# Mixture-of-experts layer on Trainium2: one wide expert and two small ones interleaved by weight halves

## The reference

```python
logits = t @ w_router + b_router
top_vals, top_idx = lax.top_k(logits, 2)
gates = sum(one_hot(top_idx, 8) * softmax(top_vals)[..., None], axis=1)
for e in range(8):
    out += gates[:, e:e+1] * ((silu(t @ w_gate[e]) * (t @ w_up[e])) @ w_down[e])
```

## Time and profile before

| | |
|---|---|
| runs | 1678.63, 1679.26, 1683.75 us (median 1679.26) |
| profiled execution | 1676.72 us, span 1675.0 us |
| TensorE | 1592.3 us busy, mean granted clock 0.973 |
| VectorE, ScalarE | 1271.2 us, 1008.1 us |
| read from HBM | 461.15 MB, 276 GB/s over the span |
| narrow items | 7, from 559.6 us on |
| wide item | matmuls from 1439.6 to 1653.7 us |

### The profile page before, as it was taken

The page is one execution under the profiler, slowest core; times in us unless marked ns, Lnnn a source line. Parts: engine busy times, 40 slices in busy tenths (PEclk is TensorE's granted clock), DMA queues, the critical chain, the costliest instruction groups (busy, mean ns, idle before and its releaser), DMA issues.

```text
span 1675.0 us, 24350 instructions
## 1 busy us (share of the span) xinstructions
PE 1592.3 (95%) x9043; PEld 1346.6 (80%) x9043; DVE 1271.2 (76%) x1389; ACT 1008.1 (60%) x1010; POOL 217.0 (13%) x251
## 2 busy tenths in 40 slices
PE   6988999997989799999999999999999999899996
PEld 4766899997678688888888888888888888788785
DVE  4895476656864898898898898888988988555454
ACT  4555555453134677777777877777776876444442
POOL 0770155531930000000000000000000000000000
PEclk9998999998999899999999999999999999999998
DMA  9954386664666699999999999999999996466531
GB/s 300 339 202 141 124 283 215 214 215 161 241 212 224 249 356 372 341 365 368 339 364 371 349 344 380 341 355 378 337 361 369 338 366 223 142 210 203 199 126 38
DMA packets 231196, 463.16 MB, mean 277 GB/s; under 512 B 18255, under 2 KB 57687, under 8 KB 231127
## 3 DMA queue, kind: packets, MB, share of 16 engines
q1 hardware_dynamic: 229591, 461.55, 77.9%
q10 hardware_dynamic: 1536, 0.68, 0.2%
HBM read 461.15 MB, written 1.05 MB: 276 GB/s over the span
## 4 chain that ended last, share of the span: by engine, by line
PE 85%; DVE 5%; POOL 4%; ACT 3%; DMA 1%; issue 1%; SPq 1%; ACTq 0%; DVEq 0%; POOLq 0%
PE bank L1984 16%; PE bank L1981 16%; PE bank L1987 16%; PE bank L1641 11%; PE bank L1796 3%; PE bank L2061 2%; PE bank L2062 2%; PE bank L2069 2%; PE bank L2074 2%; PE bank L2073 2%; DVE bank L1221 2%; PE bank L1725 1%; PE bank L1947 1%; PE bank L1629 1%; PE bank L2027 1%; DMA ring<-in_mod_w_dram 1%
## 5 line engine op out<-in xcount | busy, mean ns | idle before, releaser
L1492 DVE TENSOR_TENSOR wlo<-ring,whi 128x2048 fp32r<-128x2048 f32 x294 | 667.7, 2289 | 95.1 <-PE bank L1987 76.8
L981 ACT ACTIVATE whi<-ring 128x2048 fp32r<-128x2048 f32 x294 | 561.2, 1918 | 163.7 <-PE bank L1984 163.6
L1981 PE MATMUL bank<-whi,xe_hi 128*128 128x512 f32 x784 | 307.3, 392 | 5.4 <-ACT whi L981 5.4
L1984 PE MATMUL bank<-whi,xe_lo 128*128 128x512 f32 x784 | 306.7, 391 | 0.0
L1987 PE MATMUL bank<-wlo,xe_hi 128*128 128x512 f32 x784 | 209.8, 390 | 0.0
L1981 PEld LDWEIGHTS bank<-whi,xe_hi 128*128 128x128 f32 x784 | 147.8, 189 | 36.2 <-issue 5.6
L1984 PEld LDWEIGHTS bank<-whi,xe_lo 128*128 128x128 f32 x784 | 147.9, 189 | 30.5
L1987 PEld LDWEIGHTS bank<-wlo,xe_hi 128*128 128x128 f32 x784 | 147.6, 188 | 30.6
L1552 DVE TENSOR_TENSOR wlo<-ring,whi 128x2048 fp32r<-128x2048 f32 x42 | 96.2, 2292 | 95.1 <-PE bank L2074 94.2
L1981 PE MATMUL bank<-whi,hh 128*128 128x512 f32 x392 | 157.4, 402 | 0.0
L1984 PE MATMUL bank<-whi,hl 128*128 128x512 f32 x392 | 153.4, 391 | 0.0
(11 more groups left out here) (408 smaller groups left out, 2535.4 us busy)
## 6 DMA issues: line engine op xcount, KB each, us to landing
ring<-in_moe_w_gate_dram SPq DMA_DIRECT2D x112, 1024.0 KB, 7.2
ring<-in_moe_w_up_dram SPq DMA_DIRECT2D x112, 1024.0 KB, 7.2
ring<-in_moe_w_down_dram SPq DMA_DIRECT2D x112, 1024.0 KB, 6.9
ring<-in_mod_w_dram SPq DMA_DIRECT2D x24, 2048.0 KB, 10.0
ring<-in_ffn_w_gate_dram SPq DMA_DIRECT2D x11, 1024.0 KB, 6.4
ring<-in_ffn_w_up_dram SPq DMA_DIRECT2D x11, 1024.0 KB, 8.8
ring<-in_ffn_w_down_dram SPq DMA_DIRECT2D x11, 1024.0 KB, 5.0
ring<-in_conv_w_pw_dram SPq DMA_DIRECT2D x8, 1024.0 KB, 11.8
```

Source lines behind the costliest of these rows:

```text
L981: act.activation(whi[:, n % HI_SLOTS, :], ring[:, s * HW:(s + 1) * HW], ACT.Copy).then_inc(hi_ready, 1)
L1492: v.tensor_tensor(wlo[:, n % LO_SLOTS, :], ring[:, s * HW:(s + 1) * HW], whi[:, n % HI_SLOTS, :].bitcast(F32), ALU.subtract).then_inc(lo_r ...
L1981: mm(o[:, :], xh, hi[:, w:w + 512], start=first, stop=False)
L1984: ins = mm(o[:, :], xl, hi[:, w:w + 512], start=False, stop=False)
```

## The change

The wide item becomes a trio: the wide expert and two experts of at most 64 rows, interleaved by halves.

- The order `TRIO` has 126 halves. Two halves of a small expert and one wide half alternate; at four places there are two such pairs, at four none. The small experts follow one another (expert "1", then "2"), each as U, D of the block before, G. The wide one goes U, G for all blocks, then D. The three experts share `ring` with 6 slots (`TRIO_SLOTS`), `whi` and `wlo`.
- A small expert's rows lie like the wide one's last rows: high parts in columns 0 to 63, low parts in 64 to 127 (`xs`, and `hs` for hidden values). A half has 4 steps of 2 matmuls (with `whi`, with `wlo`), 8 in all.
- The halves of a PSUM result (partitions 0 to 63 and 64 to 127) are no longer added by `fold` on TensorE: ScalarE copies the upper 64 partitions to SBUF (`uT`, `gT`, `uBt`, `gBt`), VectorE adds the lower ones (`sums`), ScalarE takes Silu in place and VectorE multiplies (`hidden_rows`); then TensorE transposes (`transposes`, two halves after the gate block's end), ScalarE makes the high part (`act_high`) and VectorE the low one (`dve_low`).
- The small experts' rows are gathered after the first wide half (`small_gather`), their selections transposed then too. The first small expert's output is scattered during the trio, the second's before the last wide half, where TensorE waits for `wide_yl`.
- The router picks the first fitting expert and the first two small ones, expert 0 excepted, and takes the trio only if all three exist; otherwise all run as narrow items. It has nine more small operations.
- At the end the order of the last output's operations changes, and an `Abs_reciprocal_sqrt` on two values is put ahead of the wait for `acc`.

```diff
-            with sp.If(wide > 0):
-                e = sp.value_load(order_i[0:1, bass.ds(narrow, 1)], min_val=0, max_val=NE - 1)
-                for n in range(NH):
-                    sp.wait_ge(lo_ready, last * NH + (NH + n + 1 - (RAW_SLOTS if n < WIDE_SLOTS else WIDE_SLOTS)))
-                    half(e, n, WIDE_HALVES, WIDE_SLOTS)
+                three = [sp.value_load(order_i[0:1, bass.ds(row + k, 1)], min_val=0, max_val=NE - 1) for k in range(3)]
+                for q, (o, kind, j, h) in enumerate(TRIO):
+                    sp.wait_ge(lo_ready, last * NH + (NH + q + 1 - (RAW_SLOTS if q < TRIO_SLOTS else TRIO_SLOTS)))
+                    half(three[o], kind, j, h, q % TRIO_SLOTS)
...
+def trio_halves():
+    wide = [(0, kind, j, h) for j in range(FT) for kind in "UG" for h in range(2)]
+    wide += [(0, "D", j, h) for j in range(FT) for h in range(2)]
+    pairs, out = small_pairs(), []
+    for n, w in enumerate(wide):
+        take = 2 if n in (14, 28, 33, 35) else 0 if n < 2 or n in (NH - 3, NH - 1) else 1
+        for _ in range(take):
+            e, kind, j = pairs.pop(0)
+            out += [(e, kind, j, 0), (e, kind, j, 1)]
+        out.append(w)
...
+            def small_product(q, i, e, kind, j, h):
+                pe.wait_ge(hi_ready, i * NH + (q + 1))
+                hi, lo = whi[:, q % HI_SLOTS, :], wlo[:, q % LO_SLOTS, :]
+                steps = small_steps(e, kind, j, h)
+                for k, (o, x, w, first, last) in enumerate(steps):
+                    if k == len(steps) - 1:
+                        pe.wait_ge(lo_ready, i * NH + (q + 1))
+                    ins = mm(o[:, :], x, hi[:, w:w + 512], start=first, stop=False)
+                ins.then_inc(hi_used, 1)
+                for o, x, w, first, last in steps:
+                    ins = mm(o[:, :], x, lo[:, w:w + 512], start=False, stop=last)
+                ins.then_inc(lo_used, 1)
...
+            def hidden_rows(q, i):
+                o, kind, j = AFTER[q]
+                if o == 0:
+                    v.wait_ge(s_ready, i * FT + (j + 1))
+                    if j:
+                        v.wait_ge(trio_t, GI[(0, j - 1)])
+                    v.tensor_tensor(hid_e[:, :], silu_g[:, :], uA[:, :], ALU.mult).then_inc(he_ready, 1)
+                sums(q, i)
...
+                v.wait_ge(sum_silu, GI[(o, j)])
+                v.tensor_tensor(a_, a_, b_, ALU.mult).then_inc(sum_hid, 1)
...
+                    if q in T_AT:
+                        transposes(T_AT[q], i)
+                    if q == SMALL_END[2] + 1:
+                        pe.wait_ge(wide_y, 4)
+                        for m in range(4):
+                            small_scatter(2, m, psum[SPARE_BANKS[m]])
...
+            act.activation(fin_scrap[:, :], ones[:, 0:2], ACT.Abs_reciprocal_sqrt)
+            act.wait_ge(acc_half, wide * 12 + NCOMB)
```

More of the change, by code:

```diff
@@ L158 @@
 GATHER_AFTER = {AT[("D", FT - 3, 1)]: 0, AT[("D", FT - 2, 1)]: 1}
-MIN_NARROW, MAX_NARROW = NE - 1, NE + 2
+MIN_NARROW, MAX_NARROW = NE - 3, NE + 3
 MAX_ROWS = NE + 4
 TAIL = 64
[L164 to L173, removed]
@@ L174, with small_pairs @@
-SPARE_BANKS = (0, 2, 6, 7)
-WIDE_EXTRA = (1, 3, 5, 4)
-WIDE_OUT = (1, 5, 3, 4)
+TRIO_SLOTS = 6
+def small_pairs():
+    first = [(1, "U", 0), (1, "G", 0)]
+    for j in range(1, FT):
+        first += [(1, "U", j), (1, "D", j - 1), (1, "G", j)]
+    second = [(2, "G", 0)]
+    for j in range(1, FT):
+        second += [(2, "U", j), (2, "D", j - 1), (2, "G", j)]
+    return first + [(2, "U", 0), (1, "D", FT - 1)] + second + [(2, "D", FT - 1)]
+def trio_halves():
[8 more added lines that the diff above has]
+        out.append(w)
+    assert not pairs
+    return out
@@ L178 @@
+T_AT = {QEND[x] + T_OFFSET[x]: x for x in G_ENDS}
+assert len(T_AT) == len(G_ENDS) and list(T_AT.values()) == G_ENDS
+UA, UB, GA, GB, SG, SU, SD = 0, 2, 6, 7, 1, 3, (5, 4)
+SPARE_BANKS = (SG, SU) + SD
+WIDE_EXTRA = SPARE_BANKS
+WIDE_OUT = (UA, UB, GA, GB)
+SMALL_END = {e: QEND[(e, "D", FT - 1)] for e in (1, 2)}
+assert SMALL_END[2] == NQ - 3
 MAGIC = 1.5 * 2.0 ** 23
@@ L516, in _, with half @@
                     sp.dma_start(early(n, 4)[:, 0:2, :], src.rearrange("(k p) n -> p k n", p=P)).then_inc(a, 16)
[L518 to L521 removed]
+            def half(e, kind, j, h, s):
                 e1 = bass.ds(e, 1)
@@ L1403, in _ @@
             link(v.tensor_scalar(r(10), r(10), -1000.0, None, ALU.add))
[L1405 to L1408, removed]
+            over, member, fits, small = rt[:, 0, 0, :], rt[:, 0, 1, :], rt[:, 1, 0, :], rt[:, 1, 1, :]
+            upto, uptosmall, first, two = rt[:, 3, 0, :], rt[:, 3, 1, :], rt[:, 4, 0, :], rt[:, 4, 1, :]
+            gone, rest, keep, uptorest = rt[:, 2, 0, :], rt[:, 2, 1, :], rt[:, 6, 0, :], rt[:, 7, 0, :]
+            tail, main, place_3 = rt[:, 7, 1, :], rt[:, 8, 0, :], rt[:, 8, 1, :]
+            any_fit, there, without, narrow = (rt[:, 5, 0, n:n + 1] for n in range(4))
             link(v.tensor_scalar(over, psum[6][:, 256:256 + NE], float(P), None, ALU.is_gt))
             link(v.tensor_scalar(fits, psum[6][:, 256:256 + NE], float(P + TAIL), None, ALU.is_le))
+            link(v.tensor_scalar(small, psum[6][:, 256:256 + NE], float(TAIL), None, ALU.is_le))
             v.wait_ge(consts, 6)
@@ L1423, in _ @@
[L1423 to L1428 removed]
+            link(v.scalar_tensor_tensor(two, uptosmall, 2.0, small, ALU.is_le, ALU.mult))
@@ new lines, in _ @@
+            link(v.tensor_scalar(without, rt[:, 2, 0, NE - 1:NE], -1.0, float(NE), ALU.mult, ALU.add))
+            link(v.tensor_tensor(narrow, without, rt[:, 7, 0, NE - 1:NE], ALU.add))
+            link(v.tensor_tensor(main, iota_e[:, :], gone, ALU.subtract))
+            link(v.tensor_tensor(place_3, two, uptosmall, ALU.mult))
+            link(v.scalar_tensor_tensor(place_3, place_3, narrow, main, ALU.add, ALU.subtract))
+            link(v.tensor_tensor(place_3, place_3, member, ALU.mult))
```

483 lines of the change are left out of this document (324 added, 159 removed).

## The result

The changed kernel takes 1614.4 us (1611.6 to 1618.5) against 1679.0 us, a ratio of 0.9615 with a 95% interval of 0.9599 to 0.9632; forecast were 1615 us and a range of 1592 to 1648. Timed again on another chip it gave 0.9612 (0.9598 to 0.9625). The profiled execution took 1611.64 us, its span is 1608.9 us.

A forecast was written before the change was run, and what follows sets the result against it. TensorE was taken to bound both stages. Trio work of 367.3 us plus 29.5 us of stalls replaces 460.8 us, gaining 64.0: 1676.7 becomes 1612.7 us profiled, with 2.5 us for the median 1615 us; range 1592 to 1648 us.

The forecast's parts named there:

- TensorE's work: In the trio: wide and small halves, transposes, gathers, scatters and a slow-clock start, 367.3 us without stalls.
- rival 4: In the trio the queue is the bound, holding 340 GB/s: about 1625 to 1640 us; chance 0.06.
- rival 2: In the trio loads average out over the buffers, stalls under 15 us: 1585 to 1600 us; chance 0.15.
- The stalls: In the trio, TensorE's holes worked out by the order of instructions: 29.5 us in all.
- Wide gates: End of a wide gate block: a 5.1 us chain against 3.6 us of TensorE work, 1.5 us late, 7 times, 10.5 us.
- small gates: End of a small gate block: sum, Silu and product outlast the gap, 0.5 us late, 14 times, 7 us.
- double pairs: Four places with four small halves in a row: VectorE 9.2 us against TensorE 7.3, 1.9 us late each, 7.5 us.
- the steady unit: Two small halves and a wide one: the second small low part, 2.29 us, fits in 2.5 us, 0.2 us to spare.
- The pause before the last wide half: Before the last wide half TensorE waits for the second small output's low parts: 2.5 us.
- rival 3: In the trio gaps pass 2.2 us and the clock falls: 27 us more, 1642 us; chance 0.18.
- The ring: Six load slots in the trio: a load has 11 us against a median 7.2 us to land, so it is covered.
- Router and end: Nine more router operations before the first high part cost 1.8 us; the reordered end saves 1.9 us; together 0.

The follow-up runs named there:

- experiment 1: Changed kernel with a third matmul in each step of a small half (12 instead of 8, no packing gain): 1662.4 us.
- 3: Changed kernel with only half the columns of each small half's low part made: 1590.0 us.
- 2: Changed kernel with only half of each small half's 1 MB loaded: 1613.0 us.
- 4: Changed kernel in a coarser order, two wide halves and then four small ones: 1628.8 us.
- early: Changed kernel with a small gate block's copy and sum made one half earlier: 1606.2 us, ratio 0.9567 to the kernel before.
- experiment 5: Changed kernel with its halves not interleaved, packing kept: 1745.9 us.
- experiment 6: Changed kernel with a ring of three slots in the trio instead of six: 1718.0 us.
- allthree: Changed kernel with wide gate row sums before hid_e, wide transposes three halves behind, small gate copy and sum one half earlier: 1605.8 us, ratio 0.9558 to the kernel before.

## Why the prediction was right

The mechanism held, and the time, 1614.4 us against 1615, is nearer than the terms deserve: several were off by 2 to 5 us, and two waits that the trace shows had no price at all. They happened to cancel.

**What bounds.** Right. TensorE's work plus holes behind VectorE: experiments 1 and 3 show the two parts, 2 rules out the queue (rival 4), 4 and 3 rule out an averaging over the buffers (rival 2).

**TensorE's work.** A small half takes 1.81 us, 1274.17 to 1275.98 in the trace, as forecast (1.82). The 64-row transposes cost 0.32 us for four instead of 0.48, so the transposes are 28 x 0.12 + 84 x 0.08 = 10.1 us instead of 13.4. The small gathers took 3.7 us; forecast were 4.0, by luck: the earlier trace rows has 16 such products in 1.98 us, not 8, and the trio makes 32 of them, not 16. Their eight transposes took 0.9 us (1.0), and the first wide halves ran at 0.72 of the clock from 1193 to 1199, 1.7 us lost as forecast. The work is thus about 364 us against 367.3.

**VectorE.** 346 us in the trio against 358 to 363. Its low parts take the 283 us of the lower forecast; the additions are 63 us where I had 75, in part because operations one behind the other start 0.61 us apart (1265.65 and 1266.26 above) and not the 0.68 us of their rows.

**The stalls.** 396.4 - 364 = 32 us against 29.5: the sum holds better than its terms.
- Wide gates: 7 waits of 1.7 us on the weight loads, 11.9 us, against 10.5. Right, and so was the chain behind it.
- Low parts: 20.9 us in 39 waits on the weight loads, against 7 us at the small gates and 7.5 at the double pairs. Behind a wait the next load comes sooner (1302.41 to 1302.52, 0.11 us instead of 0.227) and gives part of it back; so counted, the low parts delay the stream by about 15 us. The sum holds, its parts don't:
  - Twenty-two waits of 0.38 or 0.39 us, 8.4 us and about 5 us of delay, are ones in which VectorE had stood idle ahead of the low part. It waited for the end of the wide half, and no sum or split stood in its way:

```profile
1299.57 0.39 PE L2270 MATMUL bank<-wlo,xb 128*128 128x512 f32 x1
1300.07 2.29 DVE L1744 TENSOR_TENSOR wlo<-ring,whi 128x2048 fp32r<-128x2048 f32 x1 [1.73 <-PE bank L2270]
1302.41 0.19 PEld L2302 LDWEIGHTS bank<-whi,xs 128*128 128x128 f32 x1 [0.39 <-DVE wlo L1744]
```

  This is the step of the prediction that failed: the steady unit was to have 0.2 us to spare and cost nothing. I had started the low part together with the first small half. It starts 0.50 us after the wide half's last matmul and that small half's first weight load (both 1299.57), so it is made 2.79 us after them, where TensorE asks for it after 2.5 us.
  - The four double pairs: 4.8 us in eight waits against 7.5. Six waits are of 0.5 us, as the two here; at two of the places the first of them is 0.6 and 1.1 us:

```profile
1513.54 0.19 PEld L2302 LDWEIGHTS bank<-whi,xs 128*128 128x128 f32 x1 [0.51 <-DVE wlo L1744]
...
1515.74 0.19 PEld L2302 LDWEIGHTS bank<-whi,xs 128*128 128x128 f32 x1 [0.52 <-DVE wlo L1744]
```

  I had let VectorE begin the run of four with nothing made ahead (9.2 us against 7.3); the first low part is made while the wide half still runs, so that three remain, 6.9 us against the 3 x 1.82 + 0.7 = 6.2 us after which TensorE asks for the last.
  - Behind the small gate blocks: six waits of 0.6 to 1.6 us, 5.9 us, against 14 of 0.5; taking that work out of the way there (`early`) gave 5.1 us. The last three of the 39, 1.8 us, come behind sums, splits and outputs of other blocks.
- Small transposes (L2318): 5.4 us in 19 waits for which the profile names no cause, and 1.2 us in two for `gT`. The prediction has no term for them.
- The start, priced at 2 us: TensorE waited for nothing behind the first wide half and its gathers.
- The pause before the last wide half: 0.73 us against 2.5. The outputs were read out (`y_exp`, 1579.20) while the wide half before it ran; their low parts followed behind a weight's low part from 1582.60, and TensorE began at 1583.40 with the first of them.

**Clock.** No stall fell under rival 3: the longest wait of TensorE between two halves is 1.7 us, and the clock is 1.00 from 1205 to 1587. The gaps of 2.17 us and more that it fell behind in the earlier trace rows didn't come. Experiments 5 and 6, with waits of TensorE of up to 6.4 and 4.2 us, show what comes with them: mean clocks of 0.89 and 0.91. But the length of a gap isn't a sure sign, and the margin was not as clear as I had it: see the last section.

**The ring.** Six slots cover, three don't (experiment 6). Landing took a median of 6.9 to 7.2 us in the trio, as in the earlier trace rows.

**Router and end.** The router's list is right: from the table load before it to the one behind it ScalarE's rows are 13.2 us apart before (546.37 and 559.59) and 15.0 after (545.87 and 560.89), +1.8 us. The +1.3 us above has 0.5 us less from the stages ahead in it. -2.4 and -0.6 us against -1.9 for the end. The table load did move: ScalarE does it at 1594.53 while TensorE scatters.

**What was worth what.** 49 us of the 64 come from the packing (experiment 1), in the interleaved order; in the one order without interleaving that was run (experiment 5) the kernel is slower than before. My reading is that the interleaving buys the room on the queue and VectorE, and the cover for the chain of hidden rows, in which the saved matmuls show. A third low buffer, which the 22 waits of the steady unit ask for, was not tried.

## What to carry to other kernels

When two stages are bound by the same engine but one of them leaves the others idle, interleaving alone moves little (18 us here, experiment 1); it pays by what it then allows, here a form of the small product with a third fewer matmuls: 1.82 us a half, where VectorE needs 2.29 us for the low part of one. Add up each engine's work for the mix, and where several come near the same sum, follow the order of instructions over one unit: with two or three buffers the holes come from single chains that don't fit between two halves, and they can be priced from durations in the trace. Count a buffer as free when the last matmul's row ends and the wait is passed, here 0.5 us after that matmul's start: a margin of 0.2 us in a unit that repeats forty times was none. Moving work earlier (5.1 us) gave more here than moving the consumer later (2.6 us); expect less than the waits' sum when the waited-for engine is itself nearly full. And compare stages, not whole times, where the trace allows it.

## What the runs showed that I had not expected

- A queue busy for 89% was no bound: 214 and 320 GB/s gave the same stage time (experiment 2).
- A product of 64x512 on GpSimd took 2.15 us in the mean in the trio against 1.27 us for the four of L634 in an early stage of the same kernel.
- The length of a gap doesn't tell by itself whether the clock falls. With the ring of three slots, two idle gaps of TensorE in the timeline and the windows behind them:

```profile
1274.04 0.46 PE L2318 MATMUL bank<-ident,gT 64*128 64x64 f32 x4 [2.10 <-DVE gT L1668]
...
1287.01 0.50 PE L2302 MATMUL bank<-whi,hs 128*128 128x512 f32 x1 [2.31 <-DVE wlo L1744]
...
1276.00:1284.00 8.00, 7.76 (x34) 6.44 (x35) 5.01 (x4) 4.77 (x4) 0.00 (x0) 1.00 0.80 291
1288.00:1292.00 4.00, 3.41 (x13) 2.06 (x13) 3.23 (x4) 2.43 (x2) 0.00 (x0) 0.50 0.81 262
```

  After 2.10 us the clock stayed at 2.4 GHz, after 2.31 us it was at 1.2 GHz. That looks like a limit between the two, but `allthree` has a gap of 2.45 us with the full clock behind it:

```profile
1464.00 0.47 PE L2272 MATMUL bank<-whi,hhW 128*128 128x512 f32 x1 [2.45 <-DVE hb L1692]
...
1464.00:1466.00 2.00, 2.00 (x9) 1.65 (x10) 2.00 (x2) 1.38 (x2) 0.00 (x0) 1.00 1.01 399
```

  And the coarser order has a fall behind a stretch in which no wait of TensorE, by its matmuls or its weight loads, was longer than 1.7 us, though there were several close together:

```profile
1475.00:1479.00 4.00, 2.70 (x15) 1.51 (x13) 3.23 (x3) 3.49 (x3) 0.00 (x0) 1.00 0.82 262
1479.00:1483.00 4.00, 3.82 (x10) 3.04 (x11) 4.00 (x5) 3.42 (x4) 0.00 (x0) 0.57 0.63 219
```

  So the changed kernel's seven waits of 1.7 us left the clock up in both of its traces, but rival 3 was nearer than a count of gaps above 2.2 us says.
